# Opening of a two-layer diffusion step: the last k tile's modulation moved from TensorE to VectorE

## The reference, cut to what matters

```python
def rms_norm(x, g):
    x32 = x.astype(jnp.float32)
    y = x32 * lax.rsqrt(jnp.mean(x32 * x32, axis=-1, keepdims=True) + EPS)
    return y.astype(x.dtype) * g
def modulation(cond, w_mod, b_mod):
    m = jax.nn.silu(cond) @ w_mod + b_mod
    return m.reshape(cond.shape[0], 1, N_MOD, D_MODEL)
def modulate(x, g, shift, scale):
    return rms_norm(x, g) * (1.0 + scale) + shift
def swiglu(h, w_in, w_out):
    g, u = jnp.split(h @ w_in, 2, axis=-1)
    return (jax.nn.silu(g) * u) @ w_out
# first lines of a layer; m[0] is the shift, m[1] the scale
x = x + m[2] * (0.5 * swiglu(modulate(x, norm_g[0], m[0], m[1]), w_in[0], w_out[0]))
```

## Time and profile before

| what | us |
|---|---|
| median of 3 runs (1523.96 to 1524.03) | 1523.98 |
| profiled execution, whole time | 1524.24 |
| its span, first to last instruction | 1522.0 |
| TensorE busy in it | 1512.6 (99%) |
| VectorE busy | 1083.4 (71%) |
| ScalarE busy | 665.6 (44%) |

### The profile page before, as it was taken

One profiled execution on the slowest core, in us unless ns is written; L12 is line 12 of the kernel. 1 busy time (PEld: TensorE's weight loads), 2 busy tenths in 40 slices (PEclk: granted clock), 3 DMA queues, 4 the chain that ended last, 5 costly groups with the idle time before them and its releaser, 6 DMA issues.

```text
span 1522.0 us, 21931 instructions
## 1 busy us (share of the span) xinstructions
PE 1512.6 (99%) x8864; PEld 1445.8 (95%) x8864; DVE 1083.4 (71%) x1751; ACT 665.6 (44%) x1026; POOL 18.3 (1%) x25
## 2 busy tenths in 40 slices
PE   9999999999999999999999999999999999999999
PEld 5999999978779999999999999999997899999999
DVE  5887887787687887776678787886588876443332
ACT  5433332354686633333363333325458755333221
POOL 0000000000021000000000000000000000000000
PEclk9999999999999999999999999999999999999999
DMA  9756566533224365655445565653331033333233
GB/s 392 277 213 229 212 227 213 178 138 128 81 70 166 125 229 201 245 189 189 166 178 203 212 229 199 242 187 132 115 116 56 1 126 124 138 112 139 98 132 118
DMA packets 51700, 255.91 MB, mean 168 GB/s; under 512 B 6544, under 2 KB 8848, under 8 KB 36496
## 3 DMA queue, kind: packets, MB, share of 16 engines
q1 hardware_dynamic: 49056, 251.43, 46.0%
q10 hardware_dynamic: 2544, 3.09, 0.6%
HBM read 251.72 MB, written 2.77 MB: 167 GB/s over the span
## 4 chain that ended last, share of the span: by engine, by line
PE 93%; DVE 3%; ACT 2%; DMA 1%; issue 1%; SPq 0%; ACTq 0%; DVEq 0%
PE ps L1998 29%; PE ps L2000 28%; PE ps L1999 28%; PE ps L2657 1%; PE ps L2373 1%; DMA wm_first<-in_w_mod_first 1%; PE ps L2680 1%; PE ps L2399 1%; PE ps L2666 1%; PE ps L2544 1%; DVE w_lo L1227 1%; PE ps L2123 0%; PE ps L2339 0%; PE ps L2146 0%; PE ps L2386 0%
## 5 line engine op out<-in xcount | busy, mean ns | idle before, releaser
L1227 DVE TENSOR_TENSOR w_lo<-w_raw,w_hi 128x2048 fp32r<-128x2048 f32 (+3 forms) x178 | 349.6, 1965 | 233.9 <-ACT w_hi L677 233.4
L1998 PE MATMUL ps<-hx_hi,w_hi 128*128 128x384 f32 (+1 forms) x1432 | 480.1, 335 | 0.0
L1999 PE MATMUL ps<-hx_lo,w_hi 128*128 128x384 f32 (+1 forms) x1432 | 478.6, 334 | 0.0
L2000 PE MATMUL ps<-hx_hi,w_lo 128*128 128x384 f32 (+1 forms) x1432 | 478.5, 334 | 0.0
L677 ACT ACTIVATE w_hi<-w_raw 128x2048 fp32r<-128x2048 f32 (+3 forms) x178 | 294.6, 1656 | 409.4 <-DMA w_raw<-in_w_out 218.0
L1998 PEld LDWEIGHTS ps<-hx_hi,w_hi 128*128 128x128 f32 x1432 | 268.9, 188 | 2.0 <-issue 1.8
L1999 PEld LDWEIGHTS ps<-hx_lo,w_hi 128*128 128x128 f32 x1432 | 268.9, 188 | 0.0
L2000 PEld LDWEIGHTS ps<-hx_hi,w_lo 128*128 128x128 f32 x1432 | 268.8, 188 | 0.0
L2000 PE MATMUL ps<-g_hi,w_lo 128*128 128x384 f32 x704 | 236.6, 336 | 0.0
L1998 PE MATMUL ps<-g_hi,w_hi 128*128 128x384 f32 x704 | 236.5, 336 | 0.0
L1999 PE MATMUL ps<-g_lo,w_hi 128*128 128x384 f32 x704 | 236.5, 336 | 0.0
(11 more groups left out here) (269 smaller groups left out, 1468.0 us busy)
## 6 DMA issues: line engine op xcount, KB each, us to landing
w_raw<-in_w_in SPq DMA_DIRECT2D x88, 1024.0 KB, 4.8
wm<-in_w_mod SPq DMA_DIRECT2D x128, 512.0 KB, 5.7
w_raw<-in_w_out SPq DMA_DIRECT2D x64, 704.0 KB, 4.1
w_raw<-in_w_qkv SPq DMA_DIRECT2D x12, 1024.0 KB, 4.7
wm_first<-in_w_mod_first SPq DMA_DIRECT2D x8, 1024.0 KB, 19.5
w_raw<-in_w_o SPq DMA_DIRECT2D x8, 1024.0 KB, 4.9
w_raw<-in_w_qup SPq DMA_DIRECT2D x8, 576.0 KB, 3.8
w_raw<-in_w_down SPq DMA_DIRECT2D x6, 704.0 KB, 4.1
```

Source lines behind the costliest of these rows:

```text
L1227: nc.vector.tensor_tensor(w_lo[:, slot, 0:width], w_raw[:, slot, 0:width], w_hi[:, slot, 0:width].bitcast(F32), ALU.subtract).then_inc(w_l ...
L1998: nc.tensor.matmul(out, l_hi, r_hi, start=first, stop=False)
L1999: nc.tensor.matmul(out, l_hi, r_lo, start=False, stop=False)
L2000: return nc.tensor.matmul(out, l_lo, r_hi, start=False, stop=last)
```

## The change

The shift and scale columns of k tile 7 no longer come through TensorE. A new input `w_mod_seven` (128 partitions x 2 x 1024, 1 MB) holds their weights transposed, in the place of the eighth block of `wm_first`, and VectorE forms the columns in four multiply-and-sum instructions (`last_columns`) of 128x1024, for two conditions and two blocks: three after `h_low(4)`, one after `h_low(5)`. `cond` is loaded right after wm_first 4, followed by `w_mod_seven`; ScalarE's Silu of `cond` is done in two halves around the work on tile 4. TensorE's list loses `mod_rows(7)` and `mod_columns(7)`, has `plain(1, 1, 1)` and panel 0's tiles of k = 2 ahead of `mod_rows(3)`, and from there all four tiles of a k between two modulation steps; panel 0's tiles of k = 6 and 7 come before panel 1's.

```diff
-            for k in range(KD):
+            for k in range(KD - 1):
                 sp.dma_start(wm_first[:, k], d["w_mod_first"][k]).then_inc(wmf_loaded[k], 16)
                 if k == 0:
                     load(0, "in", 0, 0)
                 elif k == 2:
                     load(1, "in", 0, 1)
+                elif k == 4:
+                    sp.dma_start(cond[:], d["cond"]).then_inc(cond_in, 16)
+                    sp.dma_start(wm_seven, d["w_mod_seven"]).then_inc(seven_in, 16)
             load(2, "in", 0, 2)
-            sp.dma_start(cond[:], d["cond"]).then_inc(cond_in, 16)
...
+                def conditions(c):
+                    act.wait_ge(cond_in, 16)
+                    nc.scalar.activation(cond[:, c, :], cond[:, c, :], ACT.Silu).then_inc(cond_ready, 1)
                 for k in range(3, KD):
-                    copied(k)
+                    if k < KD - 1:
+                        copied(k)
+                    if k == 4:
+                        conditions(0)
                     to_tile(k)
                     h_high(0, k)
+                    if k == 4:
+                        conditions(1)
...
-            act.wait_ge(cond_in, 16)
-            nc.scalar.activation(cond[:], cond[:], ACT.Silu).then_inc(cond_ready, 1)
...
                 def gains_of(k):
-                    v.wait_ge(first_mods, k + 1)
-                    gain(nc.vector.tensor_tensor(modc[:, k:k + KD + 1:KD, :],
-                                                 ps[:, first_bank(k), 0:4].rearrange("p (s c) -> p s c", s=2),
-                                                 bmod[:, k:k + KD + 1:KD, :], ALU.add))
+                    cols = modc[:, k:k + KD + 1:KD, :]
+                    if k < KD - 1:
+                        v.wait_ge(first_mods, k + 1)
+                        cols = ps[:, first_bank(k), 0:4].rearrange("p (s c) -> p s c", s=2)
+                    else:
+                        v.wait_ge(seven_step, 4)
+                    gain(nc.vector.tensor_tensor(modc[:, k:k + KD + 1:KD, :], cols, bmod[:, k:k + KD + 1:KD, :],
+                                                 ALU.add))
                     one_plus_scale(0, 0, slice(k, k + 1))
+                def last_columns(c, s):
+                    v.wait_ge(seven_in, 16)
+                    v.wait_ge(cond_ready, c + 1)
+                    if c or s:
+                        v.wait_ge(seven_step, 2 * c + s)
+                    q = KD * s + KD - 1
+                    nc.vector.scalar_tensor_tensor(seven_prod, wm_seven[:, s, :], 1.0, cond[:, c, :], ALU.mult, ALU.mult,
+                                                   accum_out=modc[:, q, c:c + 1]).then_inc(seven_step, 1)
...
                     h_low(0, k)
+                    if k == 4:
+                        last_columns(0, 0)
+                        last_columns(0, 1)
+                        last_columns(1, 0)
+                    elif k == 5:
+                        last_columns(1, 1)
...
                     plain(1, 1, 0)
-                    mod_rows(3)
                     plain(1, 1, 1)
-                    mod_columns(3)
                     tile(0, 2, 0)
                     tile(0, 2, 1)
+                    mod_rows(3)
                     tile(1, 2, 0)
+                    mod_columns(3)
                     tile(1, 2, 1)
                     mod_rows(4)
                     tile(0, 3, 0)
                     mod_columns(4)
                     tile(0, 3, 1)
+                    tile(1, 3, 0)
+                    tile(1, 3, 1)
                     mod_rows(5)
-                    tile(1, 3, 0)
+                    tile(0, 4, 0)
                     mod_columns(5)
-                    tile(1, 3, 1)
+                    tile(0, 4, 1)
+                    tile(1, 4, 0)
+                    tile(1, 4, 1)
                     mod_rows(6)
-                    tile(0, 4, 0)
+                    tile(0, 5, 0)
                     mod_columns(6)
-                    tile(0, 4, 1)
-                    mod_rows(7)
-                    tile(0, 5, 0)
-                    mod_columns(7)
-                    for half in range(2):
-                        tile(1, 4, half)
                     tile(0, 5, 1)
                     for half in range(2):
-                        tile(0, 6, half)
-                    for half in range(2):
-                        tile(0, 7, half)
-                    for k in range(5, KD):
+                        tile(1, 5, half)
+                    for k in (6, 7):
+                        for half in range(2):
+                            tile(0, k, half)
+                    for k in (6, 7):
                         for half in range(2):
                             tile(1, k, half)
```

More of the change, by code:

```diff
@@ L256, in build_step @@
         squares_all = wm[:].rearrange("p a b -> p (a b)")[:, 0:KD * T].rearrange("p (k t) -> p k t", k=KD)
+        wm_seven = wm_first[:, KD - 1].rearrange("p a b -> p (a b)").rearrange("p (s i) -> p s i", s=2)
+        seven_prod = wm_first[:, 0].rearrange("p a b -> p (a b)")[:, 0:D]
         rowm = mod_prod[:, 0:512].rearrange("p (b o) -> p b o", b=2)
@@ L275, in build_step @@
         panel_used = sem("panel_used")
-        wmf_loaded = [sem(f"wmf_loaded{i}") for i in range(KD)]
+        wmf_loaded = [sem(f"wmf_loaded{i}") for i in range(KD - 1)]
+        seven_in = sem("seven_in")
+        seven_step = sem("seven_step")
         condT_in = sem("condT_in")
@@ L1969, in _ @@
             first_norm()
-            v.wait_ge(cond_ready, 1)
+            v.wait_ge(cond_ready, 2)
             ffn_in(0)
@@ L2779 @@
         "condT": np.stack([A(c_ctx).reshape(D), A(c)[0].reshape(D)]).reshape(2, KD, P).transpose(2, 1, 0),
-        "w_mod_first": A(w_mod)[0][:, 0:2 * D].reshape(KD, P, 2, KD, P).transpose(3, 1, 0, 2, 4).reshape(KD, P, KD, 2 * P),
+        "w_mod_first": A(w_mod)[0][:, 0:2 * D].reshape(KD, P, 2, KD, P).transpose(3, 1, 0, 2, 4)
+                        .reshape(KD, P, KD, 2 * P)[0:KD - 1],
+        "w_mod_seven": A(w_mod)[0][:, 0:2 * D].reshape(D, 2, KD, P)[:, :, KD - 1].transpose(2, 1, 0),
         "w_mod": A(w_mod).reshape(DEPTH, D, 72, P).transpose(0, 2, 3, 1).reshape(MODS, P, D)[FIRST_MODS:],
```

## The result

Median 1527.38 us (12 executions, 1526.73 to 1530.43) against 1524.05 (12, 1523.96 to 1524.84). The ratio is 1.0023, 95% interval 1.0015 to 1.0030. The forecast was 1526.8, range 1524.7 to 1527.7, so the median lies in the range and 0.6 above the forecast. The changed kernel's times spread over 3.7 us where the kernel before spreads over 0.9. The four highest executions (1528.37 to 1530.43) have a mean granted clock under 1.000; the other eight have 1.000 and lie within 1526.73 to 1527.76, with a median of 1526.93. The profiled execution took 1528.37 with a span of 1526.6 and clock 0.999. It is one of the four, and this must be kept in mind when it is read.

What follows compares the result with a forecast made beforehand. TensorE, busy 99% of the span, was taken as the bound. Saving 1.70 us against waits of 0.74, 0.84, 0.65, 0.80 and 1.0 to 1.3, plus about 0.2, gave +2.8: 1523.98 becomes 1526.8 us, range 1524.7 to 1527.7.

Steps and rivals of the forecast that it cites:

- What the change saves, and the loops: Opening: TensorE saves 1.70 us; VectorE-ScalarE loops add waits of 0.74 (k = 3), 0.65, 0.80 and 1.0 to 1.3 (k = 7).
- The wait before `tile(0,3,0)`: Opening, k = 3: TensorE wants the tile at 29.34, its h lets it start at 30.08, 0.74 us of wait.
- The wait before k = 5: Opening: `tile(0,5,0)` wanted at 38.48 starts at 39.13 because three sums delay `gains_of(5)`, 0.65 us.
- The late load: Opening: wm_first 5 lands two blocks later, at 33.65, so TensorE waits 0.84 us and `mod_rows(5)` starts at 33.70.
- The sums: VectorE, opening: sums 1.15 us apart from 33.42, three of them putting `gains_of(5)` at 36.87.
- the rule cited: Trainium skill, DVE Perf Modes: a VectorE sum costs 1.23 us start to start, giving +3.05 in all; the trace's 1.15 was preferred.
- End of the opening: After `tile(0,7,0)`, 6 tiles take 3.25 us; panel 2 starts at 47.98 to 48.30 against 45.35, taken as +2.8 us.
- The late `to_tile(7)`: ScalarE, k = 7: `to_tile(7)` may come 0.58 after `gmul` instead of 0.25, putting `tile(0,7,0)` at 45.05 instead of 44.73.
- Panel 3: After panel 2: load lands 50.9 to 53.2, `w_lo` 55.1 to 57.4, wanted at 56.5; nothing added, upper end 0.9; it limits gains.
- From the opening to the time: Whole kernel: nothing later makes up the delay, so the opening's +2.8 is added to the median 1523.98, giving 1526.8 us.
- The step that was mis-sized is the clock: Rival 5: TensorE's clock falls to 1.2 GHz in the waits; each 5 us at that level costs 2.5; chance 0.02.

Runs made afterwards that it cites:

- the small sums with the old loads: Changed kernel with each VectorE sum at 8 columns instead of 1024, reading other data, loads and Silu back in the old order: 1524.47 us.
- the skipped k = 7: Kernel before without mod_rows(7), copied(7) and mod_columns(7), in its own order, k = 7 taking the columns of k = 6: 1523.83 against 1524.08 us.
- the second's: The unaltered changed kernel run once more, beside the order-only kernel (kernel before with the changed TensorE list alone) on one chip: 1526.80 us.
- three kernels: Zero matmuls in the order-only kernel's long wait, 1526.48; in all four waits of the changed kernel, 1526.69; in three waits with panel 1's k = 6 tiles first, 1526.50.
- the one kernel with unfilled waits: Changed kernel with panel 1's two tiles of k = 6 ahead of panel 0's tiles of k = 7, nothing filled: 1526.71 us.
- one wait filled on another chip: Changed kernel with two matmuls of zeros before mod_rows(5), where TensorE waits for wm_first 5: 1529.32 us (6 executions).
- the pair above: Order-only kernel (kernel before with the changed TensorE list alone), executions with and without a clock fall; tile(0,7,0) to panel 2 took 4.74 and 3.25 us.

## Why the prediction was right, and where it was not

- *What the change saves, and the loops.* The loop from `mod_columns` to the tile of its own k was 2.85 in the prediction; after, 26.57 to 29.41 = 2.84, 41.21 to 44.06 = 2.85. The wait before `tile(0,3,0)` was 0.74 forecast and 0.7 found. Confirmed by the small sums with the old loads: order and loops alone give back more than the 1.70. The wait before k = 5, forecast 0.65, is hidden by the slow clock in the first profile; where the clock held it is 0.2 to 0.7.
- *The late load.* `mod_rows(5)` at 33.70 forecast, 34.26 found. TensorE was ready 0.7 sooner than thought (0.4 of it stands already at 20.49, against 20.87 in the kernel before) and the block landed 0.6 later, so this wait was 2.1 instead of 0.84. It cost no more time than forecast, as the sums end at the same place, but it is the wait behind which the clock fell in the first profile.
- *The sums.* 1.15 each was too small: the three took 1.36, 1.80 and 1.19. About 0.2 of each of the first two goes with the wait for the one just before; the other 0.45 of the second is open. `gains_of(5)` was nevertheless at 37.04 against 36.87, because the sums began 0.73 sooner. That two errors cancel here is luck. As to the rule cited, 1.23 from start to start: the runs have 1.34 with such a wait and 1.15 without it; neither is the rule's figure, though its length of one instruction, 1.22 to 1.23, holds.
- *End of the opening.* 6 tiles in 3.25, panel 2 at 47.98 to 48.30: found 48.17 and 48.12 where the clock held. The late `to_tile(7)` is in both.
- *Panel 3* did not wait: its load came after 5.2 us, at 53.0, and 8.32 lie between the two starts. That it caps a gain is shown by the skipped k = 7, but the cap is not fixed at 53.4: it moved to 52.8 when the load was asked for sooner.
- *From the opening to the time.* The prediction added its 2.8 to the whole time and so took the 2.24 us beside the span as unchanged. They fell by 0.4, while the span of the executions at full clock grew by 3.0 to 3.2, more than the 2.8 of the opening. The two nearly cancel, which is luck: by its span alone the forecast is 0.2 to 0.4 low. Neither was traced.
- *The step that was mis-sized is the clock.* "Between 10 and 15 us TensorE was busy for only 3.95 of 5 us, and the granted clock stayed at 1.00, so only 0.02". The price was about right and the chance was not: one execution was taken for all. The clock fell in 4 of 12 executions and in 2 of 11, also in that very stretch, and the two profiled cases cost 1.5 us each. It is 1527.38 - 1526.93 = 0.45 in the first set's median, most of the 0.6 by which it lies above the forecast, and 0.15 in the second's. With the waits filled the clock was 1.000 in all 33 executions of three kernels. That the waits bring the falls behind them is likely, but not shown: all three ran on one chip, on which the one kernel with unfilled waits had no fall either, and with one wait filled on another chip it still fell in 3 of 6. Why it also fell at 10 to 15 us, ahead of the waits, in one profiled execution is open.

A rule that I left out bears on this. The Trainium skill, TensorE: Matmul & The Clock Gate, section "HAM oscillation — how this bites in real kernels", says that idle gaps between matmuls throttle TensorE and the next matmuls start cold. The traces agree in part. Falls came behind waits of 1.1, 1.8 and 2.0 us, in some executions and not in others. But the next matmuls did not start slow: they ran at full clock for another 0.3 to 1.9 us before it fell.

## What to carry to other kernels

Low busy time of an engine is no room if that engine is half of a serial loop with another: measure the loop, and count how much of the bound engine's work lies between its start and its use. Before removing work from the bound engine, look for what is late next, at each of the following steps; here the load, the next panel's `w_lo` and the one after it all stood within a microsecond. New waits of one or two microseconds on TensorE can cost more than their length, in some executions only, and a fall of the clock behind them can cost nothing where further waits follow: compare times at equal granted clock. Filling the wait with idle matmuls is worth a try, beside the unfilled kernel on the same chip.

## What the runs showed of the hardware that was not expected

- After waits of 1.1, 1.8 and 2.0 us in the opening the granted clock fell to 1.2 GHz in some executions of one kernel and not in others. The first slow matmul came 0.3 us (44.62 behind 44.34), 1.9 us (40.71 behind 38.77) and 1.3 us (35.55 behind 34.26, 45.85 behind 44.52) after the restart. One fall cost 1.49 us in the pair above, and another, in front of two waits, nothing.
- A VectorE sum that waits on a semaphore for the instruction just before starts 1.34 us after it, one that waits for the instruction before that 1.15, which is less than its own length of 1.22.
- The 1 MB `kvv_raw` load left ScalarE idle for 2.95 and 2.78 us in two executions and for 1.1 to 1.2 in others, at the same place of the program. The two lost 1.2 and 0.8 us there.
